# Prompt thirds of branch products 1 and 2 issued inside the sample tiles' chains, and the first splits of the feed-forward reordered

## What is computed

```python
xn = rms_norm(x, g_mix_pre)
q, k, v, o, ig, fg, glu, xq, gates = split(xn @ w_in)
y_ml = rms_norm_per_head(mlstm(q, k, v, ig, fg, state)) * g_mhead * sigmoid(o)   # 4 heads x 256, matrix memory
y_cv = silu(layer_norm(causal_dwconv(glu)))
y_xa = mem_attention(xq, mk, mv)              # 256 memory tokens; the samples have caches of their own
mixed = (sigmoid(gates[0]) * (y_ml @ w_branch[0]) + sigmoid(gates[1]) * (y_cv @ w_branch[1])
         + sigmoid(gates[2]) * (y_xa @ w_branch[2]))
x = x + rms_norm(mixed @ w_out, g_mix_post)
fa, fb = split(rms_norm(x, g_ffn_pre) @ w_ffn_in)
x = x + rms_norm((silu(fa) * fb) @ w_ffn_out, g_ffn_post)
```

## Time and profile before

| | |
|---|---|
| median of three runs | 2720.0 us |
| the profiled execution | 2721.45 us, span 2719.7 us |
| busy share: TensorE, weight loads, VectorE, ScalarE, GpSimd | 97%, 92%, 40%, 23%, 24% |
| mean granted clock of TensorE | 0.992 |
| L259, the units of projection and branches | 3 x 2496 matmuls, about 334 ns each in the pipeline |
| L247 (hi) and L251 (lo), one unit's weights | 1052 and 2663 ns in the mean |
| DMA | 293.99 MB, mean 108 GB/s |

### The profile page before, as it was taken

One profiled execution on the slowest core, in us unless ns is written; L12 is line 12 of the kernel. 1 busy time (PEld: TensorE's weight loads), 2 busy tenths in 40 slices (PEclk: granted clock), 3 DMA queues, 4 the chain that ended last, 5 costly groups with the idle time before them and its releaser, 6 DMA issues.

```text
span 2719.7 us, 36585 instructions
## 1 busy us (share of the span) xinstructions
PE 2631.9 (97%) x14872; PEld 2503.2 (92%) x14872; DVE 1096.6 (40%) x1299; ACT 623.6 (23%) x904; POOL 642.6 (24%) x320
## 2 busy tenths in 40 slices
PE   6999999999999999999998997999999999999998
PEld 5999999999999999998888986978999999989897
DVE  5420399999952222216643442444121111111115
ACT  5221111111113233214421141133201111202021
POOL 6312122222211211222201120420412222314031
PEclk9999999999999999999999998999999999999999
DMA  7422333334252222354475654432201111102013
GB/s 228 125 83 88 124 112 125 108 124 135 92 182 83 89 91 92 123 165 121 122 220 180 212 185 172 130 119 83 70 24 47 47 47 39 55 24 63 24 32 139
DMA packets 270017, 293.99 MB, mean 108 GB/s; under 512 B 10954, under 2 KB 228386, under 8 KB 269888
## 3 DMA queue, kind: packets, MB, share of 16 engines
q1 hardware_dynamic: 258012, 245.00, 29.0%
q10 hardware_dynamic: 11884, 47.35, 4.3%
HBM read 208.27 MB, written 84.50 MB: 108 GB/s over the span
## 4 chain that ended last, share of the span: by engine, by line
PE 62%; issue 28%; POOL 5%; DVE 2%; ACT 1%; DMA 1%; PEld 0%; ACTq 0%; POOLq 0%; PEldq 0%; DVEq 0%; SPq 0%
PE PS L259 22%; PE PS L2006 20%; PE PS L2029 10%; POOL w_lo L251 4%; PE PS L1976 3%; PE PS L1257 1%; PE PS L1265 1%; PE PS L1595 1%; PE PS L1576 1%; PE PS L1221 1%; DVE A_lo L558 0%; PEld PS L495 0%; PE PS L1239 0%; DVE y_T L1423 0%; PE PS L1216 0%
## 5 line engine op out<-in xcount | busy, mean ns | idle before, releaser
L259 PE MATMUL PS<-A_hi,w_hi 128*128 128x384 f32 x2496 | 574.8, 335 | 7.6 <-POOL A_lo L1730 4.4
L259 PE MATMUL PS<-A_lo,w_hi 128*128 128x384 f32 x2496 | 572.4, 334 | 0.0
L259 PE MATMUL PS<-A_hi,w_lo 128*128 128x384 f32 x2496 | 572.4, 334 | 0.0
L251 POOL TENSOR_TENSOR w_lo<-w_raw,w_hi 128x1024 fp32r<-128x1024 f32 x120 | 319.3, 2663 | 1047.0 <-ACT w_hi L247 1046.9
L259 PEld LDWEIGHTS PS<-A_hi,w_hi 128*128 128x128 f32 x2496 | 445.9, 188 | 10.4 <-issue 6.8
L259 PEld LDWEIGHTS PS<-A_lo,w_hi 128*128 128x128 f32 x2496 | 446.0, 188 | 0.0
L259 PEld LDWEIGHTS PS<-A_hi,w_lo 128*128 128x128 f32 x2496 | 446.0, 188 | 0.0
L944 DVE SCALAR_TENSOR_TENSOR c_out<-ext,taps,c_out 128x1024 f32<-128x1024 f32 x480 | 424.1, 958 | 0.9 <-DVE c_out L944 0.9
L247 ACT CAST w_hi<-w_raw 128x1024 fp32r<-128x1024 f32 x120 | 126.1, 1052 | 1058.5 <-PE PS L259 1049.7
L2006 PE MATMUL PS<-A_hi,w_hi 128*128 128x384 f32 x1056 | 242.4, 334 | 2.8 <-POOL w_lo L1921 2.8
L2006 PE MATMUL PS<-A_lo,w_hi 128*128 128x384 f32 x1056 | 242.2, 334 | 0.0
(11 more groups left out here) (292 smaller groups left out, 2585.4 us busy)
## 6 DMA issues: line engine op xcount, KB each, us to landing
proj_d<-stage ACTq DMA_DIRECT2D x80, 576.0 KB, 2.7
w_raw<-in_w_in SPq DMA_DIRECT2D x80, 512.0 KB, 4.1
w_raw<-in_w_ffn_in SPq DMA_DIRECT2D x44, 512.0 KB, 3.8
w_raw<-in_w_branch SPq DMA_DIRECT2D x24, 512.0 KB, 4.7
w_raw<-in_w_ffn_out SPq DMA_DIRECT2D x22, 512.0 KB, 3.5
glu<-proj_d SPq DMA_DIRECT2D x16, 576.0 KB, 5.9
gate_in<-proj_d SPq DMA_DIRECT2D x16, 576.0 KB, 6.1
part_d<-part_out SPq DMA_DIRECT2D x16, 576.0 KB, 4.9
```

The lines of the kernel that those rows point to most:

```text
L251: nc.gpsimd.tensor_tensor(w_lo[:, s % SPLIT, 0:kt], w_raw[:, s, 0:kt], w_hi[:, s % SPLIT, 0:kt].bitcast(F32), ALU.subtract).then_inc(w_lo_ ...
L259: last = nc.tensor.matmul(out, w[:, k], m(k, c), start=start and k == 0 and n == 0, stop=stop and k == kt - 1 and n == 2)
```

## The change

- **Two units' prompt thirds inside the sample chains.** Thirds 0 and 1 of units 0 and 1 of branch products 1 and 2 become `early_part`s, issued by TensorE within the sample tile's chain. mLSTM: unit 0's two thirds behind `final_state(1)`, unit 1's behind all turns; `y_turn(SB)` moves behind `final_state(3)` and to banks 6 and 7, and ScalarE's `hi(SB)` behind the last copy of the final states. Cross-attention: unit 0's two thirds ahead of the turn of the probabilities, one third of unit 1 behind the value products and one behind the last turn. `pe_branch` then issues the two last thirds and six whole units.
- **Banks.** In product 1 the two bank groups swap their roles; in the cross-attention the scores move to banks 4 to 7 and turns and outputs to 0 to 3, except for the sample tile's turn (6 and 7).
- **Loops** of TensorE's branch products are written out.
- **Feed-forward.** ScalarE and GpSimd split the weights of units 0 and 1 after `scale_x` of tiles 0 and 1, and `mix_his(1)` goes ahead; SP loads two of six early jobs in the tile loop; TensorE's order at the start is unit 0 thirds 0, 1; unit 1 third 0; unit 0 third 2; unit 1 thirds 1, 2.

```diff
+        def br_banks(n, s):
+            return banks((s + n) % 2 if n < 2 else s % 2)
+        def early_part(pe, n, s, c):
+            pe.wait_ge(w_lo_done, U_BR + KT * n + s + 1)
+            return product([br_banks(n, s)[c]], w_hi[:, s], w_lo[:, s], lambda k, _: a_hi(k, c), lambda k, _: a_lo(k, c), KT)
...
         def pe_branch(pe, n, ready, count):
...
+            pe.wait_ge(ready, count)
+            for s in range(2):
+                early_part(pe, n, s, 2).then_inc(w_used, 1)
+            for j in range(2, KT):
+                J = KT * n + j
+                pe.wait_ge(part_done, J - 1)
+                use_unit(pe, U_BR + J, j, br_banks(n, j), a_hi, a_lo)
...
             final_state(0)
             final_state(1)
-            y_turn(SB, 0)
+            pe.wait_ge(sc_new, NB * H)
+            pe.wait_ge(ml_lo, 8)
+            early_part(pe, 1, 0, 0)
+            pe.wait_ge(ml_num, H * (SB + 1))
+            pe.wait_ge(ml_lo, 14)
+            early_part(pe, 1, 0, 1)
             final_state(2)
             final_state(3)
+            pe.wait_ge(nu_new, 1)
+            y_turn(SB, 0)
             pe.wait_ge(fc_copied, H)
+            early_part(pe, 1, 1, 0)
+            early_part(pe, 1, 1, 1)
+            pe.wait_ge(nf_copied, 3)
...
             for h in range(H):
-                if h == 2:
-                    hi(SB)
                 act.wait_ge(fc_turn, h + 1)
                 nc.scalar.copy(fc_out(h), PS[:, h % 2].rearrange("p (z d) -> p z d", z=2)).then_inc(fc_copied, 1)
+            hi(SB)
...
             pe.wait_ge(part_mul, KT - 1)
             scores(0, 0, 0)
+            scores(1, 1, 0)
             pe.wait_ge(part_mul, KT)
-            scores(1, 1, 0)
             p_turn(0, 0)
...
             pe.wait_ge(ck_a, NB)
+            pe.wait_ge(ck_d, NB)
+            pe.wait_ge(xa_lo, 2 * 3)
+            early_part(pe, 2, 0, 0)
+            pe.wait_ge(xa_lo, 2 * 6)
+            early_part(pe, 2, 0, 1)
             p_turn(SB, 0)
             pe.wait_ge(xa_copied, SB + 1)
-            pe.wait_ge(ck_d, NB)
             pe.wait_ge(cv_own, 1)
...
+            early_part(pe, 2, 1, 0)
             pe.wait_ge(cv_nat, 1)
...
             last.then_inc(cv_turned, 1)
+            pe.wait_ge(xa_exp, SB + 1)
+            early_part(pe, 2, 1, 1)
...
-            for n in range(U_F + KT, U_F + KT + 6):
+            for n in range(U_F + KT, U_F + KT + 4):
                 load_job(sp, n)
...
                 if t + 1 < NT:
                     load_x(sp, t + 1)
+                if t < 2:
+                    load_job(sp, U_F + KT + 4 + t)
...
             in_unit(0, (0, 1), False)
             turn_x(NT - 1)
-            in_unit(1, (0, 1), False)
+            in_unit(1, (0,), False)
             in_unit(0, (2,), True)
-            in_unit(1, (2,), True)
+            in_unit(1, (1, 2), True)
...
             mix_his(0, 1)
-            hi_job(act, IN_JOB[0])
-            hi_job(act, IN_JOB[1])
+            mix_his(1, 0)
+            mix_his(1, 1)
             for t in range(NT):
-                if t + 1 < NT:
+                if 0 < t < NT - 1:
                     mix_his(t + 1, 0)
                     mix_his(t + 1, 1)
...
                 scale_x(t)
+                if t < 2:
+                    hi_job(act, IN_JOB[t])
...
-            lo_job(pool, IN_JOB[0])
-            lo_job(pool, IN_JOB[1])
             for t in range(NT):
                 power_y(t)
                 power_x(t)
+                if t < 2:
+                    lo_job(pool, IN_JOB[t])
```

More of the change, by code:

```diff
@@ L1042, in pool_branch @@
                     unit(s // RAW, s % RAW)
-        def pe_branch(pe, n, ready, count):
[L1045 to L1065, removed]
+        def br_banks(n, s):
+            return banks((s + n) % 2 if n < 2 else s % 2)
@@ new lines, in early_part, with pe_branch_0 @@
+        def early_part(pe, n, s, c):
+            pe.wait_ge(w_lo_done, U_BR + KT * n + s + 1)
+            return product([br_banks(n, s)[c]], w_hi[:, s], w_lo[:, s], lambda k, _: a_hi(k, c), lambda k, _: a_lo(k, c), KT)
+        def pe_branch_0(pe):
+            for s in range(2):
+                pe.wait_ge(p_copied, NPROJ - 1 + s)
+                if s == 0:
+                    pe.wait_ge(ln_lo, 1)
+                    early_part(pe, 0, s, 0)
+                    pe.wait_ge(ln_lo, 2)
+                    early_part(pe, 0, s, 1)
+                    pe.wait_ge(ln_lo, 3)
+                    early_part(pe, 0, s, 2).then_inc(w_used, 1)
+                else:
+                    use_unit(pe, U_BR + s, s, br_banks(0, s), a_hi, a_lo)
+            for j in range(2, KT):
+                pe.wait_ge(part_done, j - 1)
+                use_unit(pe, U_BR + j, j, br_banks(0, j), a_hi, a_lo)
@@ L1067, in dve_branch @@
+        def pe_branch(pe, n, ready, count):
+            pe.wait_ge(ready, count)
+            for s in range(2):
+                early_part(pe, n, s, 2).then_inc(w_used, 1)
+            for j in range(2, KT):
+                J = KT * n + j
+                pe.wait_ge(part_done, J - 1)
+                use_unit(pe, U_BR + J, j, br_banks(n, j), a_hi, a_lo)
         def dve_branch(dve, n, between=None):
@@ L1241, in y_turn @@
             def y_turn(t, b):
+                bank = 6 if isinstance(t, int) and t == SB else 2
                 pe.wait_ge(ml_y, t + 1)
@@ L1245, in y_turn @@
                         k = 4 * n + q
[L1246 removed]
+                        last = nc.tensor.transpose(PS[:, bank + n, P * q:P * (q + 1)], oy[:, b, k // 2, P * (k % 2):P * (k % 2 + 1)], ident[:])
                     last.then_inc(ml_yT, 1)
@@ L1575, in scores @@
                     for z in range(2):
-                        last = nc.tensor.matmul(PS[:, 2 * b + h // 2, MEM * (h % 2):MEM * (h % 2 + 1)], xq_in[:, b, 2 * h + z],
+                        last = nc.tensor.matmul(PS[:, 4 + 2 * b + h // 2, MEM * (h % 2):MEM * (h % 2 + 1)], xq_in[:, b, 2 * h + z],
                                                 mk_T[:, 2 * h + z], start=z == 0, stop=z == 1)
@@ L1585, in p_turn @@
                     for h in range(H):
-                        last = nc.tensor.transpose(PS[:, 4 + m, P * h:P * (h + 1)], prob[:, b, h, P * m:P * (m + 1)], ident[:])
+                        last = nc.tensor.transpose(PS[:, (6 if isinstance(t, int) and t == SB else 0) + m, P * h:P * (h + 1)], prob[:, b, h, P * m:P * (m + 1)], ident[:])
                 last.then_inc(xa_pT, 1)
@@ L1594, in out @@
                     for m in range(2):
-                        last = nc.tensor.matmul(PS[:, 6 + k // 4, P * (k % 4):P * (k % 4 + 1)], mv[:, m, P * k:P * (k + 1)],
+                        last = nc.tensor.matmul(PS[:, 2 + k // 4, P * (k % 4):P * (k % 4 + 1)], mv[:, m, P * k:P * (k + 1)],
                                                 prob_T[:, b, m, k // 2], start=m == 0, stop=m == 1)
@@ L1643, in k_scores @@
                     for h in range(H):
-                        last = nc.tensor.matmul(PS[32 * h:32 * (h + 1), p // 2, MEM * (p % 2):MEM * (p % 2 + 1)], own_q[:, b, 2 * h + z],
+                        last = nc.tensor.matmul(PS[32 * h:32 * (h + 1), 4 + p // 2, MEM * (p % 2):MEM * (p % 2 + 1)], own_q[:, b, 2 * h + z],
                                                 ck_T[b % 2][:, 2 * h + z], start=b % 4 == 0 and z == 0, stop=b % 4 == 3 and z == 1,
@@ L1686, in turned @@
                     act.wait_ge(xa_y, t - 1)
-                nc.scalar.copy(prob_T[:, b].rearrange("p m h j -> p m (h j)"), PS[:, 4:6]).then_inc(xa_copied, 1)
+                nc.scalar.copy(prob_T[:, b].rearrange("p m h j -> p m (h j)"), PS[:, 6:8] if isinstance(t, int) and t == SB else PS[:, 0:2]).then_inc(xa_copied, 1)
             def hi(t):
@@ L1715, in act_xattn @@
                     act.wait_ge(ck_used, b - 1)
-                nc.scalar.copy(ck_T[b % 2][:, 0:4].rearrange("p (a k) m -> p a (k m)", a=2), PS[:, 4:6]).then_inc(ck_a, 1)
+                nc.scalar.copy(ck_T[b % 2][:, 0:4].rearrange("p (a k) m -> p a (k m)", a=2), PS[:, 0:2]).then_inc(ck_a, 1)
             act.wait_ge(ck_used, NB)
```

16 lines of the change are left out of this document (8 added, 8 removed).

## The result

The changed kernel takes 2698.3 us against 2722.2 us of the kernel before on the same chip, a ratio of 0.9912 (95% interval 0.9899 to 0.9924), 24 us less. The forecast was 2698, within 2688 to 2707.

The account below looks back on a forecast made before the run. TensorE, busy 97% of the span, was taken as the bound, so time could come only from its waits and low clock. Gains of 9.3 + 4.0 + 6.3 + 2.8 = 22.4 us gave 2698 us, range 2688 to 2707.

Parts of the forecast that it names:

- The four steps: Gains: mLSTM tail 9.3 us, cross-attention sample tile 4.0, feed-forward tile 1 6.3, feed-forward unit 2 2.8.
- the addition behind unit 0: mLSTM tail: unit 2 of product 1 waits for part_done of unit 0, stopping TensorE 0.9 us.
- Y's landing: Product 2: Y lands 14.6 us after SP enters; unit 2 starts after a stop of 7.7 us.
- The stop ahead of the value products: Cross-attention sample tile: the uncovered chain through prob_T and the masked copy, 4.58 us, stays.
- Two slow starts: Cross-attention: low clock after stops; value matmuls take 9.3 us instead of 7.3, unit 2 of product 2 costs 2.8 more.
- VectorE beside GpSimd: Addition before unit 2 of product 2: 1.36 us with GpSimd idle; 3.42 beside its splits would make the gain 1.9.
- The bounds for the mLSTM part: mLSTM tail gain from 7 us (prev_in lands late, slow start) to 10.2 (no wait at unit 2).
- the 4.9 us: Feed-forward head: TensorE's wait for Y_lo ahead of tile 1, 4.9 us, goes once mix_hi precedes the weight splits.
- (a): Product 2: Y loads do not hold unit 2; 9.6 us more gain, 2688 us; chance 12%.
- (b): Feed-forward head: wait only moves to tile 2; 5 us less and the 2.8 lost, 2705 us; chance 13%.
- (c): Delayed sample chains eat the mLSTM and cross-attention gains, feed-forward gives 5 us, or parts wait later; 2715 us; 8%.
- (d): Product 2: clock stays low behind the new 7.7 us stop, kernel slower, 2735 us; chance 4%.

Follow-up runs that it names:

- undo_mlstm: Changed kernel with the mLSTM early parts taken back, units 0 and 1 of product 1 whole behind the wait for ml_lo: 2707.9 us, 0.9947 of before.
- mul: Changed kernel, but unit j of products 1 and 2 waits only until unit j - 2 is read out of its bank (part_mul): 2684.8 us, 0.9865 of before.
- undo_xattn_again: Changed kernel without the cross-attention early parts, timed with more rounds beside the changed kernel: 2699.9 us, 0.9920 of before.
- mid: Changed kernel with one of the two thirds ahead of the turn of the probabilities moved behind it: 2691.0 us, 0.9889 of before.
- undo_ffn: Changed kernel with the feed-forward head's loads, splits and first units in the order of before: 2706.5 us, 0.9939 of before.
- undo_third: Changed kernel with only the first two feed-forward units in the order of before: 2700.8 us, 0.9922 of before.

## Why the prediction was right

**Which limits count.** TensorE's stops and slow starts at the seams were the whole of it. The four steps were forecast at 9.3, 4.0, 6.3 and 2.8 us, and the profiles give 9.6, 4.3, 6.5 and 3.0. That each is where it was put is shown by the profiles of the kernels that undo it: each lengthens its own stretch, by 11.5 us (mLSTM part), 3.2 to 3.6 (cross-attention part), 5.2 and 4.6 (the two halves of the feed-forward part, 9.6 together), and leaves the other two within 0.7 us, but for the 1.7 us of `undo_mlstm`. So they add. The 11.5 and the 4.6 contain slow starts that the kernel before didn't have, so the prices of undoing a part are somewhat above its gain. The medians (9.5, 4.2, 4.9 and 4.1 us) agree with this within their uncertainty, and can't show it by themselves.

**What was late next.** In the mLSTM tail the addition behind unit 0, 0.9 us forecast, 0.67 measured. In product 2 Y's landing: a stop of 7.7 us forecast, 7.63 measured, from 14.8 us of transfers behind SP's entry (14.6 forecast), 1.36 us of addition and TensorE's end of work. That this stop costs what it shows is settled by `mul`; that the parts leave about 4 us is what `undo_xattn_again` shows. The stop ahead of the value products was 4.34 us, 4.58 forecast.

**The clock.** Two slow starts were charged, 2.0 us in the value products and 2.8 in unit 2. The products took 9.8 us (forecast 9.3), unit 2 to 7 took 77.10 against 75.1, so 2.0 and not 2.8. The two errors nearly cancel, which is luck. The 2.8 us came from a stop of 4.35 us; behind the longer one of 7.6 us the slow start was the cheaper, and it was 1.7 to 2.3 us in every profile that has this stop (76.75 to 77.35 us). `mid` shows the value products apart: without their stop, 7.1 us.

**VectorE beside GpSimd.** 1.36 us was taken for the addition and came. That chose between 4.0 and 1.9 us for the part, and the rule of the Trainium skill (SBUF — State Buffer, "Who interferes with whom") put it on the same side. In the changed kernel GpSimd splits weights up to 1679.22, those of unit 3 too, which the forecast had left out, and is idle from there to the addition at 1681.88.

**What was mis-sized.** Runs of one kernel spread by 1 to 6 us (2694.9 to 2696.2, `undo_ffn` 2702.5 to 2708.9), and its two profiles differ by clock stretches elsewhere, which no step had. The forecast of 2697.6 against a measured 2698.3 and 2695.7 owes part of its closeness to these and to a kernel before that came out at 2722.2 instead of 2720.0: the four steps together were right to 1 us (23.4 against 22.4), and that 2698.3 lies as near to the forecast is partly luck. The bounds for the mLSTM part (7 to 10.2) took prev_in's landing as a risk; it landed 7.3 us after its issue at 1447.32 (6.9 forecast), at 1454.6, 2.3 us ahead of the addition, about the cover of 2.4 us that had been named. For the feed-forward head the term was right, but what it rests on, the 4.9 us, isn't a constant: the same order gave 3.6 us behind the changed seams, and a slow start more at unit 2.

**The rivals.** (a), Y doesn't hold unit 2: refuted, the wait is there. (b), the wait moves one tile on: it does, with 0.3 us. (c) and (d) didn't occur; the low clock behind the 7.6 us stop was over within the first 6 us (0.65 from 1683.3 to 1689.3, then 1.00), sooner than behind the shorter stop of before (0.50 in the first 6 us).

## What to carry to other kernels

Work that fills a stop has to be followed to the next thing that the stop had been hiding: here transfers that were asked for at the same moment as before and had always been covered by the first unit. Look then at what the new wait really names; a wait on "added to the sum" where "read out of the bank" is enough cost 10 us. And put the filler behind the instruction that starts the chain, not ahead of it: the same third, moved by one instruction group, gave 5 to 6 us more.

## What the runs showed of the hardware

- Behind a stop of TensorE of 4.34 us the next 64 matmuls took 6.38 us instead of 3.66 at the full clock; behind the same stop they took 6.29 in a second profile of the same kernel and 5.35 in `undo_mlstm`. So the price of one and the same stop varies by 1 us.
- A longer stop didn't cost more: product 2 takes 2.8 us more behind 4.35 us without work (102.95 against 100.15 for 576 matmuls), and 2.0 us more behind 7.63 us (77.10 against 75.1 for 432).
- A stop of 2.8 us was followed by a slow stretch in two kernels (64.25 us for 360 matmuls in `undo_third`, 64.07 in `undo_ffn`, clock 0.72 in the first 6 us) and by none in another (62.67, before, clock 1.00).
- Behind the stops of 0.67 us at unit 2 of product 1 and 0.18 us in `mid` the clock stayed at 1.00. At 1547.21 in the changed kernel it was low behind a wait of only 0.76 us, the last of three between 1535 and 1547 (1.60, 1.44, 0.76); with 0.41 us as the last one it was 1.00 in the second profile.
- 4.6 MB asked for within 6 us landed 14.6 us after the first issue before and 14.8 us after: Y's second pair took 8.3 and 9.1 us before and 8.3 and 9.2 after.
